# All projections as plain float32 matmuls on 1 MB weight pieces, in place of halved fp32r operands on 512 KB pieces

## The reference, cut to what matters

```python
u = x @ w_in[i]                                  # 2048 x 10544
y_r = _rwkv7_mixer(u_r, ...)                     # 16 heads, recurrent
y_m = _mlstm_mixer(u_m, ...)                     # 8 heads, chunks of 128
mix = (sigmoid(g_r) * (y_r @ w_br[i]) + sigmoid(g_m) * (y_m @ w_bm[i])) @ w_out[i]
x = _layer_norm(ALPHA * x + mix, ln1_w[i], ln1_b[i])
moe = _hier_moe(x, w_rg, b_rg, w_re, b_re, w_gate, w_up, w_down)   # 32 experts, top 2
ple = sigmoid(x @ w_pg[i]) * (p[i] @ w_ple[i])
x = _layer_norm(ALPHA * x + moe + ple, ln2_w[i], ln2_b[i])
```

## Time and profile before

| | |
|---|---|
| median of 3 runs | 3741.41 us (3740.63 to 3742.02) |
| profiled execution | 3748.91 us, span 3747.2 us |
| PE busy | 3253.6 us (87%) |
| DVE, ACT, POOL busy | 1579.5, 765.5, 246.5 us |
| mean granted TensorE clock | 0.907 |
| DMA | 722.85 MB, mean 193 GB/s |

### The profile page before, as it was taken

How to read it: one execution, slowest core, us unless ns; L and a number is a source line. 1 busy time by engine, 2 the same in 40 slices (tenths; PEclk the granted TensorE clock), 3 DMA queues, 4 the chain that set the end, 5 groups by cost and what they waited for, 6 DMA issues and landing times.

```text
span 3747.2 us, 38142 instructions
## 1 busy us (share of the span) xinstructions
PE 3253.6 (87%) x16082; PEld 2263.2 (60%) x16082; DVE 1579.5 (42%) x1896; ACT 765.5 (20%) x823; POOL 246.5 (7%) x225
## 2 busy tenths in 40 slices
PE   7967887966999958999999999949999797999867
PEld 5726875855666746433333333328867677999645
DVE  3444335354233445222222222254886444444445
ACT  3320111331222313110010011000001233444222
POOL 1002220000000000000000000006340000000000
PEclk9967877976999969999999999979999997999768
DMA  5410002531554514999999999944443346888213
GB/s 193 142 52 1 1 1 66 155 90 37 171 163 156 198 62 141 394 424 425 425 425 425 425 425 425 425 188 135 119 118 113 101 148 133 185 184 188 86 34 135
DMA packets 217572, 722.85 MB, mean 193 GB/s; under 512 B 20368, under 2 KB 22544, under 8 KB 166320
## 3 DMA queue, kind: packets, MB, share of 16 engines
q1 hardware_dynamic: 213408, 698.02, 53.1%
q0 software_dynamic: 3440, 18.11, 1.4%
q10 hardware_dynamic: 544, 4.19, 0.3%
HBM read 718.16 MB, written 2.10 MB: 192 GB/s over the span
## 4 chain that ended last, share of the span: by engine, by line
PE 72%; DMA 12%; DVE 12%; ACT 2%; issue 1%; POOL 1%; DVEq 0%; ACTq 0%; POOLq 0%
PE psum L134 70%; DMA t<-in_w_up 11%; DVE t L274 8%; PE psum L140 2%; ACT t L245 2%; DVE t L285 1%; DVE t L289 1%; DMA t<-in_ln_b 1%; DVE t L260 1%; POOL t L319 1%; DVE t L281 0%; POOL t L314 0%; DVE t L279 0%; DVE t L297 0%; ACT t L247 0%
## 5 line engine op out<-in xcount | busy, mean ns | idle before, releaser
L134 PE MATMUL psum<-t,t 128*128 128x256 f32 (+10 forms) x14350 | 3033.2, 427 | 198.8 <-DVE t L274 129.6
L134 PEld LDWEIGHTS psum<-t,t 128*128 128x128 f32 (+3 forms) x14350 | 2052.4, 187 | 1144.2 <-issue 698.8
L274 DVE TENSOR_TENSOR t<-t,t 128x1024 fp32r<-128x1024 f32 (+7 forms) x626 | 763.8, 1220 | 748.1 <-ACT t L245 713.0
L245 ACT ACTIVATE t<-t 128x1024 fp32r<-128x1024 f32 (+9 forms) x494 | 491.9, 996 | 1155.7 <-PE psum L134 728.8
L274 DVE TENSOR_TENSOR t<-t,psum 128x1024 f32<-128x1024 f32 (+2 forms) x321 | 286.0, 891 | 898.3 <-PE psum L134 622.6
L245 ACT ACTIVATE t<-psum 128x1024 f32<-128x1024 f32 (+5 forms) x286 | 230.2, 805 | 1742.2 <-PE psum L134 1415.7
L140 PE MATMUL psum<-t,t 128*128 128x128 f32 (+3 forms) x676 | 123.0, 338 | 263.6 <-DVE t L274 164.3
L140 PEld LDWEIGHTS psum<-t,t 128*128 128x128 f32 (+3 forms) x676 | 98.6, 175 | 306.1 <-issue 148.8
L319 POOL TENSOR_TENSOR t<-t,t 128x1024 f32<-128x1024 f32 (+6 forms) x112 | 194.2, 1734 | 415.5 <-DVE t L274 331.5
L274 DVE TENSOR_TENSOR t<-psum,t 128x1024 f32<-128x1024 f32 (+5 forms) x129 | 107.3, 832 | 164.7 <-PE psum L134 140.4
L260 DVE COPY t<-psum 128x256 f32<-128x256 f32 (+6 forms) x91 | 56.7, 623 | 171.9 <-PE psum L140 101.1
(11 more groups left out here) (67 smaller groups left out, 194.0 us busy)
## 6 DMA issues: line engine op xcount, KB each, us to landing
t<-in_w_gate SPq DMA_DIRECT2D x128, 1024.0 KB, 17.0
t<-in_w_up SPq DMA_DIRECT2D x128, 1024.0 KB, 19.0
t<-in_w_down SPq DMA_DIRECT2D x128, 1024.0 KB, 18.0
t<-in_w_in SPq DMA_DIRECT2D x160, 512.0 KB, 4.3
t<-in_w_in_odd SPq DMA_DIRECT2D x128, 512.0 KB, 5.7
t<-in_w_in_even SPq DMA_DIRECT2D x96, 512.0 KB, 3.7
t<-in_w_out SPq DMA_DIRECT2D x32, 512.0 KB, 4.3
t<-in_w_pg SPq DMA_DIRECT2D x32, 512.0 KB, 4.3
```

Of the source, the lines that this page charges most:

```text
L134: ins = self.e.matmul(o, l, r, start=start, stop=stop, skip_group_check=True)
L245: self.put(self.e.activation(o, i, f, scale=scale), event)
L274: self.put(self.e.tensor_tensor(o, a, b, op), event)
```

## The change

All halves go. `xT` and its kin become one float32 tensor, `turned` copies the transposed inputs (banks 0 and 2 on ACT, 1 and 3 on DVE), and PE waits for `landed` instead of `halved`. The six stream buffers hold 1 MB each. `proj_a` and `proj_b` take two places (two pairs of banks) and work on 1024 columns by 256 rows at once: with one stationary operand `proj_a` makes two matmuls of 512 columns. The even block's native pieces become four k tiles by 512 columns in three of the buffers. The shift matmuls of a pair of `ur` chunks come after the next pair's projection. The router's and the gather's matmuls become plain float32. The experts get 12 slots, ten of them free before the `pl` stage ends (it was six of ten). `mi.g` and `pl.g` keep two results.

```diff
-    def piece(self, name, e, r0, kt, c0, n, rows=128, halved=True):
+    def piece(self, name, e, r0, kt, c0, n, rows=128, of=6):
...
-        self.wait_ge(("halved" if halved else "landed", w.tag, j))
-        return j, *w.views(j, spec)
+        self.wait_ge(("landed", w.tag, j))
+        return j, w.slot(j, spec)
...
-            src = w.slot(i, spec)
-            hi, lo = w.views(i, spec)
-            if self.name == "act":
-                self.wait_ge(("landed", w.tag, i), before is not None and ("used", w.tag, before) or None)
-                self.activation(hi, src, ACT.Copy, event=("hi", w.tag, i))
-            else:
-                self.wait_ge(("hi", w.tag, i), before is not None and ("used", w.tag, before) or None)
-                self.tt(lo, src, hi.bitcast(F32), ALU.subtract, event=("halved", w.tag, i))
...
+    def turned(self, key, dst, js, done):
+
+        for j in js:
+            self.wait_ge((key, j))
+            self.copy(dst[:, 4 * j:4 * j + 4, :].rearrange("p k (b t) -> p b k t", b=2),
+                      self.bank(key, j).rearrange("p (b k t) -> p b k t", b=2, k=4), event=(done, j))
+            self.free(key, j)
...
-        stream = Stream("s", bufs(6, 3), plan.get("s", []), 2, plan.get("turn", 0))
+        stream = Stream("s", [alloc(2048) for _ in range(6)], plan.get("s", []), plan.get("turn", 0))
...
-        slots = [alloc(2048) for _ in range(6)] + [at(xT_at + 2048 * k, 2048) for k in range(4)]
+        slots = [alloc(2048) for _ in range(10)] + [at(xT_at + 2048 * k, 2048) for k in range(2)]
...
-                                if split:
-                                    xh, xl = xt[0][:, g0 + k, tb], xt[1][:, g0 + k, tb]
-                                    p.mm(v[:, b, :], xh, hi[:, k, :], st, False)
-                                    p.mm(v[:, b, :], xh, lo_[:, k, :], False, False)
-                                    p.mm(v[:, b, :], xl, hi[:, k, :], False, sp, event=done)
...
+                    kt = max(k for k in (1, 2, 4, 8, 16) if KT % k == 0 and k * n <= 2048)
+                    for g0 in range(0, KT, kt):
+                        j, w = p.piece(wn, ex, 128 * g0, kt, c0 + c, n)
+                        for k in range(kt):
+                            st, sp = bias is None and g0 + k == 0, g0 + k == KT - 1
+                            for b in range(2):
+                                for ci, m in parts:
+                                    end = k == kt - 1 and b == 1 and ci == len(parts) - 1
+                                    p.mm(v[ci][:, b, 0:m], xt[:, g0 + k, 128 * b:128 * b + 128],
+                                         w[:, k, 512 * ci:512 * ci + m], st, sp,
+                                         event=("used", p.stream.tag, j) if end else None)
...
+                for c in range(0, ncols, 1024):
+                    v = [pe.take(key, c // 512 + ci).rearrange("p (m t) -> p m t", m=4) for ci in range(2)]
+                    pe.wait_ge(*after)
                     for g0 in range(0, KT, 2):
...
+                        j, w = pe.piece(wn, None, 128 * g0, 2, c0 + c, 1024)
+                        for k in range(2):
+                            for m in range(8):
+                                pe.mm(v[m // 4][:, m % 4, :], w[:, k, 128 * m:128 * m + 128], xt[:, g0 + k, :],
+                                      g0 + k == 0 and m % 2 == 0, g0 + k == KT - 1,
+                                      event=("used", "s", j) if m == 7 and k == 1 else None)
...
-                        for a_ in range(2):
-                            for b in range(2):
-                                pe.mm(ps[:, k, :], xm[a_][:, b, d0:d0 + 128], sel_[g % 2][:, b, :], a_ + b == 0,
-                                      a_ + b == 2, event=("mo.xg", g, kq) if k == 3 and a_ + b == 2 else None)
+                        for b in range(2):
+                            pe.mm(ps[:, k, :], xm[:, b, d0:d0 + 128], sel_[g % 2][:, b, :], b == 0, b == 1,
+                                  event=("mo.xg", g, kq) if k == 3 and b else None)
...
+            for cc in range(4):
+                proj_a(pe, f"ur{cc}", xT, 16, "w_in", 1024 * cc, min(1024, 3360 - 1024 * cc), ("in.xTc", 2), ("in.xTc", 3))
+                if cc:
+                    shifted(cc - 1)
+            shifted(3)
...
-                for ci in range(2):
-                    v.ahead_of("ml.o", ci)
...
-                v.wait_ge(("ev.oTh", 4 + ci))
...
-                v.wait_ge(("od.oTh",))
-                v.tt(xT[1], oTo, xT[0].bitcast(F32), ALU.subtract, event=("od.oT",))
...
-                a.wait_ge(("od.gated", 3, 1))
-                a.copy(xT[0], oTo, event=("od.oTh",))
...
+                    if name == "w_out_even_2":
+                        s.wait_ge(("ev.scored", 3), ("s5.phases", 7))
...
-                if i > 9:
-                    s.wait_ge(("used.w", i - 10))
-                elif i > 5:
-                    s.wait_ge(("pl.g3", 0))
+                if i > 11:
+                    s.wait_ge(("used.w", i - 12))
+                elif i > 9:
+                    s.wait_ge(("pl.g1", 0))
```

More of the change, by code:

```diff
@@ L8 @@
 F32 = mybir.dt.float32
-F32R = mybir.dt.float32r
 ALU = mybir.AluOpType
@@ L614, in lora @@
                 for kk_, rr_ in parts:
-                    j, sl, _ = pe.piece(wname, None, r0, 2, 0, 512, rows=rr_, halved=False)
+                    j, sl = pe.piece(wname, None, r0, 2, 0, 512, rows=rr_)
                     sls.append((j, sl, kk_, rr_))
@@ L1178, in tensor_program @@
             even()
-            proj_a(pe, "ev.out", oTr, 16, "w_out_even_2", 0, 2048, ("ev.oT",))
+            proj_a(pe, "ev.out", oT, 16, "w_out_even_2", 0, 2048, ("ev.oT",))
             pe.meet(12)
@@ L1184, in tensor_program @@
             odd()
-            proj_a(pe, "od.out", xT, 16, "w_out_odd_2", 0, 2048, ("od.oT",))
+            proj_a(pe, "od.out", oTo, 16, "w_out_odd_2", 0, 2048, ("od.gated", 3, 1))
             pe.meet(14)
@@ L1956, in vector_program @@
             route()
[L1957 to L1964 removed]
+            v.wait_ge(("mo.xm",))
+            for c in range(2):
+                for ci in range(2):
+                    cs = slice(1024 * c + 512 * ci, 1024 * c + 512 * ci + 512)
+                    v.wait_ge((f"pl.e{c}", ci), ("pl.gate", c, ci))
+                    v.tt(gsp[ci], gsp[ci], half(v.bank(f"pl.e{c}", ci)), ALU.mult)
+                    v.free(f"pl.e{c}", ci)
+                    v.stt(acc[:, :, cs], x[:, :, cs], ALPHA, gsp[ci], ALU.mult, ALU.add, event=("pl.mul", c, ci))
+                if c == 0:
                     rank()
             moe()
[L1967 removed]
             v.wait_ge(("mo.flagged",))
@@ L1980, in vector_program @@
             rms("r1", ("ev.h",), hne, rse, rwe)
-            for j in (1, 3):
-                v.wait_ge(("ev.T", j))
-                v.copy(hTe[:, 4 * j:4 * j + 4, :].rearrange("p k (b t) -> p b k t", b=2),
-                       v.bank("ev.T", j).rearrange("p (b k t) -> p b k t", b=2, k=4), event=("ev.hT", "dve"))
-                v.free("ev.T", j)
+            v.turned("ev.T", hTe, (1, 3), "ev.hT")
             even()
@@ L2314, in scalar_program @@
             route()
-            for c in range(4):
-                if c:
-                    a.wait_ge(("pl.mul", c - 1))
-                out_of(f"pl.g{c}", gsp, 0, ACT.Sigmoid, event=("pl.gate", c))
+            for c in range(2):
+                for ci in range(2):
+                    if c:
+                        a.wait_ge(("pl.mul", 0, ci))
+                    out_of(f"pl.g{c}", gsp[ci], ci, ACT.Sigmoid, event=("pl.gate", c, ci))
             moe()
-            a.limit = stream.first("w_out_even_2")
             a.wait_ge(("mo.flagged",))
@@ L2335, in scalar_program @@
                 std("r1", rse[:, 4 + b:5 + b], rse[:, 2 + b:3 + b], b)
-            for j in (0, 2):
-                a.wait_ge(("ev.T", j))
-                a.copy(hTe[:, 4 * j:4 * j + 4, :].rearrange("p k (b t) -> p b k t", b=2),
-                       a.bank("ev.T", j).rearrange("p (b k t) -> p b k t", b=2, k=4), event=("ev.hT", "act"))
-                a.free("ev.T", j)
+            a.turned("ev.T", hTe, (0, 2), "ev.hT")
             even()
-            for ci in range(4):
-                a.ahead_of("ev.out", ci)
             a.meet(12)
```

404 lines of the change are left out of this document (127 added, 277 removed).

## The result

The kernel after takes 3927.64 us (median of 4 runs, 3924.98 to 3929.57), the kernel before 3741.02 us in the same job: ratio 1.0499, 95% interval 1.0481 to 1.0517. The forecast was 3923.3 us in a range of 3890 to 3955 and slower with 0.98.

The account below looks back on a forecast made before the run. The prediction took PE as the bound (87% busy, 72% of the chain), with DMA close to it in the experts. Its terms summed to +181.9 us on 3741.4, giving 3923.3 us, range 3890 to 3955.

Parts of the forecast that it names:

- Part 1: All projections: native float32 pieces cost 0.65 us (`proj_a`) or 0.57 us (`proj_b`) more, +261.4 us; last `ur` columns +2.
- Rival 5: Projections: each of four passes bears a single one's overhead, 0.93 us per 512-column matmul; +127 us, 4050; chance 0.02.
- rival 6: Projections: successive matmuls sharing a stationary operand overlap, a `proj_a` piece taking 1.75 us; 511 less, 3412; chance 0.01.
- Part 2: Sums of few columns in `ml.if16`, `od.f16` and the router become 64 records each: -20.3 us.
- rival 2: Sums of few columns are cheap throughout, 0.117 us a record: -15 us, 3908; chance 0.09.
- Part 3: PE's waits and cold starts at `ur`, `ml.o`, mix, `pl`, turned inputs, `ev.out` and `od.out` go or shrink: 79.6 us gained.
- the rest are short waits for halves that DVE makes behind its products: Mix: stage time beyond the matmuls, bias pairs and cold start was taken as PE waits that go, -8 us.
- Part 4: Paired results end together, so the last DVE operation comes later in `mi.o`, `ev.out`, `od.out` and the mix: +6 us.
- Part 5: Experts: the native gather makes PE the bound instead of DMA, 30.20 us an expert; +12.4 us with the first gather.
- One sign that I had named: Experts: the DMA share would fall below 1.
- Rival 1: Experts stay DMA-bound and the gather's growth is hidden: -12 us, 3911; chance 0.13.
- Rivals 3 and 4: Pieces of 1 MB late at stage restarts, +20, chance 0.12; waits in `ml.o`, `pl`, mix stay, +36, chance 0.10.

Follow-up runs that it names:

- e4: The kernel before with one native float32 matmul in place of three float32r ones in every projection, halves still made and waited for: 3983.11 us, ratio 1.0634.
- e1b: The kernel after with the projections walking 512 columns at a time instead of 1024: 3916.92 us, ratio 1.0485.
- e6: e5 plus the shift matmuls of each `ur` chunk issued behind the next chunk's projection: 3722.24 us, ratio 0.9951 to the kernel before.
- e5: The kernel before with the halves of the first ten `ml.o` pieces made during the convolution: 3730.07 us, ratio 0.9965.
- e7: e6 with the halves of twelve and not ten `ml.o` pieces made early: 3718.11 us, ratio 0.9939 to the kernel before.
- e3: The kernel after with the experts' gather in float32r from the high part of x alone: 3915.86 us, ratio 1.0451 to the kernel before.
- e2: The kernel after with the mix stage's 16 one-row bias matmuls spread among full products: 3925.02 us, ratio 1.0479 to the kernel before.
- e9: The kernel after with the edits of e1b and e2 together: 3921.59 us, ratio 1.0483 to the kernel before.

## Why the prediction was right, term by term

The forecast's terms, put together by stage, beside the two spans. Each measured figure is the difference of the stage's length in the two traces.

| stage | terms | forecast | measured |
|---|---|---|---|
| `ur` | 48 x 0.65 + 2 - 7.3 | +25.9 | +23.2 |
| `ml.qk`, `ml.v`, `ml.if16` | 16 x 0.57 + 16 x 0.65 - 6.4 | +13.1 | +12.0 |
| turned inputs and starts, six places | | -9.1 | -8.7 |
| `ml.o` | 16 x 0.65 - 19 | -8.6 | -5.6 |
| mix | 64 x 0.65 - 8 + 2.4 | +36.0 | +43.6 |
| `mi.o` and its norm | 32 x 0.65 + 1.2 | +22.0 | +17.6 |
| router | | -7.0 | -6.7 |
| `pl` up to the first expert | 32 x 0.65 - 19.8 + 5 | +6.0 | +7.7 |
| experts | 12.4 - 5 | +7.4 | +8.1 |
| even block | | -8.3 | -7.1 |
| `ev.out` | 32 x 0.65 + 1.2 | +22.0 | +20.8 |
| `od.f16` | | -6.9 | -7.4 |
| `od.q` to the last attention | 96 x 0.57 + 32 x 0.65 - 8.1 | +67.4 | +62.1 |
| `od.out` | 32 x 0.65 + 1.2 | +22.0 | +20.2 |
| constants, `rwkv` | | 0 | -3.4 |
| sum | | +181.9 | +176.4 |

The last column comes from one profile of each kernel. The second profile of the kernel after is 12 us longer, 6.3 of them in the mix and some 7 in the last attention, both by the clock. So a miss of a few us in one of these rows is no finding by itself.

**Part 1 held.** The native records cost 0.427 and 0.215 us, and e4, which changes nothing but the matmuls, shows 0.635 us a piece and +238.8 us in all: this term is the whole of the loss. By the rows a 512-column matmul in float32 costs 0.857 us, 3.7 times a float32r one of 0.2317. The Trainium skill's page "FP8 and Floating Point Precision", section "TensorE Precision Notes", gives true FP32 four passes through the array. The trace agrees with it in the direction, at 3.7 and not 4. Rival 5 (each pass with the cost of a single one) falls, and so does rival 6: e1b, whose matmuls don't share a stationary tile, has the same 110.1 us in `mi.o`. The stretch from `od.q` to `od.z` grew by 77.4 us (392.44 to 469.83), 75.5 by the terms. In `ur` the last 288 columns were mis-scaled: 0.2317 x 288 / 512 is 0.13 and not 0.14, which makes the term +3 in place of +2. The stage came 2.7 us lower all the same, since moving the shifts gave 9.7 (e6) and not 7.3.

**Part 2 held** within 0.5 us in the router and the forget gate. `od.f16` takes 12.84 us and not the cheap 7.5 that rival 2 wanted for it.

**Part 3 held in all but one place.** The step that failed is "the rest are short waits for halves that DVE makes behind its products", -8 us in the mix. The trace of before has no such wait: in 902.60 to 1214.90 PE was busy for 312.28 of 312.30 us, and the only wait of the stage is 3.9 us for the bias's transfer. The stretch, with the columns of the earlier trace rows:

```profile
902.60:1214.90 312.30, 312.28 (x1056) 202.51 (x1056) 89.44 (x73) 76.17 (x72) 0.00 (x0) 0.98 0.49 157
```

I had taken the difference between the stage and its matmuls at full speed for waits. It lies in PE's own time: 64 x 2.78 + 32 x 3.43 + 13.7 is 301.4 us, the low clock takes 7.7 (low for some 9 us at the start and again behind the one-row matmuls; the forecast had 1.8 of it) and the eight groups of one-row matmuls about 3, together 312.1. The native form pays nearly the same, so taking the halves away gains nothing here. With 0 in place of the -8 the stage comes to +44.0, and it measured +43.6. `ml.o` was mis-sized: -19 became -16, since a cold start costs the native form too: the low clock took 4.2 us from the two starts of the halved form and 3.1 from the one start here (786.5 to 792 us stand at 0.50), a gain of 1.1 where I had 4. e5 to e7 test this term and the shifts' from the other side: -13 of -19 at once, -5 more by the twelve pieces in the profile, and -9.7 for -7.3.

The attention behind `od.z` came out 7.1 us shorter than I had, with nothing changed in it: 48 of its records took 17.49 us in before's profile, at a granted clock of 0.50 to 0.79, and 12.39 in after's, whose first 6.6 us stand at 1.00; in the second profile of the kernel after they took 17.46. That is chance and no gain. `mi.o` gained 4.4 that were not in the sum. 2.6 of it is the norm behind it, which waits for the load of its bias: the load stands in the chain with 9.51 us before and 6.90 after, and that it was quicker is no part of the change. The other 1.8 is the start. I had the same cold start in both, and the native form has none (first the kernel before, then after):

```profile
1225.76:1228.00 2.24, 2.24 (x5) 1.79 (x6) 0.00 (x0) 0.00 (x0) 0.00 (x0) 0.50 0.29 121
```
```profile
1291.14:1293.00 1.86, 1.86 (x5) 0.90 (x6) 0.00 (x0) 0.00 (x0) 0.00 (x0) 1.00 0.48 203
```

`od.out` starts at 0.50 before and at 1.00 after as well, which is its 20.2 for 22.0. The constants that GpSimd makes at the start are not in the forecast either: they are ready 1.7 us sooner (the first transpose starts at 16.10 and, in the second profile, 16.17, against 17.76). The other 1.7 us of that row, in `rwkv`, are absent from the second profile: its longest wait is 36.80 us before, 35.22 and 36.65 after.

**Part 4 held** in the mix (5.16 to 2.57 us in e1b). In `ev.out` the tail is covered in part by a load, as e1b showed.

**Part 5 held**: 120.97 us a group where I had 4 x 30.20 = 120.8, no wait for `w_up`, and the bound changes back when the gather is cheap (e3). One sign that I had named did not come: the DMA share did not fall below 1, it stayed at 1.01 with 420 GB/s for 425. The wait for `w_up` tells which of the two is the bound, the share does not. Rival 1 falls. Rivals 3 and 4 have no place in the profile: the only transfers that PE itself waits for in the whole span are the router's and the gates' biases (7.9 and 3.9 us), never a piece.

The errors of the mix (+7.6), `ml.o` (+3), the attention (-7.1 by the clock) and `mi.o` (-4.4) nearly cancel. The forecast of the total is better than its parts, and that is luck: one of them, the attention's -7.1, is absent from the second profile. The 181.9 lie between the 176.5 of the spans and the 186.6 of the medians. The same shows between e4 and the kernel after: e4 came 11 us under its +250 (0.015 a piece and 9 us of hidden waits would be 14), and the step from there to the kernel after was 12.7 us smaller than the 68.2, of which the mix's 8 and `ml.o`'s 3 are 11.

## What to carry to other kernels

When PE is the chain and its projections run without a gap, an edit that frees VectorE and ScalarE is worth only the waits at the joins; count those one by one, and compare the matmuls' own price by records per stretch at one granted clock. Here the larger part of two such waits could be had by reordering the queues (a few lines in e5 to e7, -0.5 to -0.6%), with no slower arithmetic. And before the difference between a stage and its matmuls is called a wait, look at PE's busy time in that very stretch: if it is whole, the difference lies in PE's own time, here the clock and the transitions to one-row matmuls. A remedy can bring its own price: spreading the bias matmuls gave back 6.9 us of clock and cost some 5 of transitions. Of two bounds that lie close together, the wait ahead of the matmuls tells which one holds; a DMA share of 1.01 stood in both.

## What the hardware showed that I had not expected

- The granted clock falls while PE is busy. Behind one-row matmuls it stood at 0.50 to 0.67 for 4 us and more with PE busy for 4.00 of 4.00 us, and the same stage of 800 records took 353.30 us or 359.58 in two profiles of one kernel. Two profiles of the same kernel differ by 12 us of span for such reasons (3923.7 and 3935.7), as much as the effects of e1b, e2 and e9.
- A one-row matmul among full ones costs 0.40 us more than its own two records, at full clock (2.97 us for six records in place of 2.57, e2); four in a row pay it once.
- Two bounds can lie within 2% of each other, and a stage then moves from one to the other with an edit of a few per cent: an expert group took 118.97 us by its transfers, 120.97 by PE, and 119.6 by its transfers again when 33 us of PE's work in 600 were taken out.
- The load of a norm's weights (1 MB written) on GpSimd's queue landed 4.8 us after its issue in one kernel and 10.5 in another that differs only in the order of its projections.
